# A hybrid attention and RG-LRU encoder layer: sixteen pairs of weight tiles in seven products, and one more high part made by ScalarE

## The reference

```python
proj = einsum('bsd,de->bse', x, w_in) + b_in          # x is 1024 x 1024
q, k, v, g_attn, x_rnn, g_rnn, m_attn, m_rnn = split(proj)
attn = window_attention(rope(q), rope(k), v, sink) * silu(g_attn)      # 8 heads, |i-j| <= 128
xc   = centred_depthwise_conv(x_rnn, conv_w, conv_b)                   # width 4, 10 blocks of 128 channels
r, i = sigmoid(xc @ wa + ba), sigmoid(xc @ wx + bx)                    # per block, two directions
a    = exp(-8 * r * softplus(-lam));  u = sqrt(1 - a*a) * i * xc
rnn  = (scan_forward(a, u) + scan_backward(a, u)) * silu(g_rnn)
merged = sigmoid(m_attn) * (attn @ w_branch_attn) + sigmoid(m_rnn) * (rnn @ w_branch_rnn)
x = layernorm(alpha * x + merged @ w_out + b_out)
```

## Time and profile before

| | us |
|---|---|
| median of 3 runs (lowest to highest) | 1029.85 (1028.64 to 1030.46) |
| the profiled execution | 1029.07 |
| its span | 1027.3 |
| TensorE, GpSimd, VectorE, ScalarE busy in the span | 1009.8, 618.0, 670.9, 471.8 |

### The profile page before, as it was taken

One profiled execution on the slowest core, in us unless ns is written; L12 is line 12 of the kernel. 1 busy time (PEld: TensorE's weight loads), 2 busy tenths in 40 slices (PEclk: granted clock), 3 DMA queues, 4 the chain that ended last, 5 costly groups with the idle time before them and its releaser, 6 DMA issues.

```text
span 1027.3 us, 12975 instructions
## 1 busy us (share of the span) xinstructions
PE 1009.8 (98%) x4641; PEld 836.1 (81%) x4641; DVE 670.9 (65%) x769; ACT 471.8 (46%) x687; POOL 618.0 (60%) x378
## 2 busy tenths in 40 slices
PE   8999999999999999999999999999999999999997
PEld 6888888888888888878887888787887878888885
DVE  4946665503556653666587886877878488839756
ACT  4054445221554465573758466574856741102021
POOL 5654435446543422535499999999999734485223
PEclk9999999999999999999999999999999999999999
DMA  8264333565524121435262534435243788937012
GB/s 330 98 240 134 126 120 113 178 239 187 168 78 163 53 71 52 143 106 192 65 218 76 154 102 136 130 115 164 84 142 84 242 296 322 341 99 295 1 47 118
DMA packets 65861, 154.69 MB, mean 151 GB/s; under 512 B 6928, under 2 KB 7312, under 8 KB 65680
## 3 DMA queue, kind: packets, MB, share of 16 engines
q1 hardware_dynamic: 56880, 131.36, 38.7%
q10 hardware_dynamic: 8928, 22.64, 5.7%
HBM read 108.88 MB, written 45.09 MB: 150 GB/s over the span
## 4 chain that ended last, share of the span: by engine, by line
PE 83%; POOL 7%; DVE 4%; issue 3%; DMA 2%; ACT 1%; SPq 0%; DVEq 0%; POOLq 0%; ACTq 0%
PE proj L863 13%; PE proj L865 13%; PE proj L864 13%; PE proj L1067 6%; PE proj L1071 5%; PE proj L1073 5%; POOL w_lo L751 5%; PE aux L863 3%; PE aux L865 3%; PE aux L864 3%; PE aux L927 3%; PE aux L909 2%; POOL w_hi L764 2%; PE proj L1184 1%; PE proj L1183 1%
## 5 line engine op out<-in xcount | busy, mean ns | idle before, releaser
L716 POOL TENSOR_SCALAR w_hi<-raw 128x1024 fp32r<-128x1024 f32 (+1 forms) x46 | 62.5, 1358 | 246.1 <-PE proj L863 190.4
L863 PE MATMUL proj<-xt_hi,w_hi 128*128 128x512 f32 x476 | 192.2, 404 | 0.2
L865 PE MATMUL proj<-xt_hi,w_lo 128*128 128x512 f32 x476 | 186.4, 392 | 0.0
L864 PE MATMUL proj<-xt_lo,w_hi 128*128 128x512 f32 x476 | 186.2, 391 | 0.0
L751 POOL TENSOR_TENSOR w_lo<-raw,w_hi 128x512 fp32r<-128x512 f32 x66 | 123.7, 1879 | 4.4
L719 POOL TENSOR_TENSOR w_lo<-raw,w_hi 128x1024 fp32r<-128x1024 f32 (+1 forms) x46 | 123.4, 2682 | 3.8
L865 PEld LDWEIGHTS proj<-xt_hi,w_lo 128*128 128x128 f32 x476 | 89.3, 188 | 19.7
L863 PEld LDWEIGHTS proj<-xt_hi,w_hi 128*128 128x128 f32 x476 | 89.6, 188 | 15.7 <-DVE xt_lo L1604 0.8
L864 PEld LDWEIGHTS proj<-xt_lo,w_hi 128*128 128x128 f32 x476 | 89.6, 188 | 14.1
L1067 PE MATMUL proj<-xt_hi,w_hi 128*128 128x512 f32 x224 | 87.8, 392 | 1.5 <-POOL w_lo L751 1.5
L1073 PE MATMUL proj<-xt_hi,w_lo 128*128 128x512 f32 x224 | 87.2, 389 | 0.0
(11 more groups left out here) (199 smaller groups left out, 2467.6 us busy)
## 6 DMA issues: line engine op xcount, KB each, us to landing
raw<-stream SPq DMA_DIRECT2D x52, 512.0 KB, 4.2
presum_a<-stream SPq DMA_DIRECT2D x42, 256.0 KB, 2.9
sums<-presum_a SPq DMA_DIRECT2D x42, 256.0 KB, 2.0
raw<-sums SPq DMA_DIRECT2D x38, 256.0 KB, 2.8
spill<-part ACTq DMA_DIRECT2D x16, 512.0 KB, 3.1
merges<-stage_out ACTq DMA_DIRECT2D x32, 256.0 KB, 3.6
raw<-stream SPq DMA_DIRECT2D x31, 256.0 KB, 2.7
raw_half<-stream SPq DMA_DIRECT2D x21, 256.0 KB, 2.8
```

What stands on the lines that cost most here:

```text
L716: nc.gpsimd.tensor_scalar(hi, raw[:, raw_slot, cols], 1.0, 0.0, ALU.mult, ALU.add)\
L863: begun = nc.tensor.matmul(bank, wh, mov_hi, start=first, stop=False)
L864: nc.tensor.matmul(bank, wh, mov_lo, start=False, stop=False)
L865: return begun, nc.tensor.matmul(bank, wl, mov_hi, start=False, stop=last)
```

## The change

`PLAIN` goes from 3 to 1. The units x3, g1, x4 and g2 become two more x/g pairs; the first pair of all is no longer a merge pair but (x3, g1), and 16 pairs are 8 x/g and 8 merge pairs. The order of the first blocks is written anew on each engine (four branch tiles before gates(1,0); in block 2 TensorE runs products 0 to 3 of its x/g pair between gates(2,0) and gates(2,1), in the later blocks product 0 alone as before). The sums of weights have 32 parts in place of 28. `BY_ACT` gets product 6 of each x/g pair, and products 2 to 6 of the very first; in the loop over blocks ScalarE makes this copy behind decay_exp and early_copy(q,2). GpSimd makes the gate weights behind product 6 for the first two x/g pairs and behind product 3 else, as before. The last loads (`load_branch(0)`, the states) wait for two more splits.

```diff
...
-PLAIN = 3
-TWINS = [(("merge", 0, 0), ("merge", 0, 1))]
+PLAIN = 1
+TWINS = []
 for _b in range(PLAIN, RNN_BLOCKS):
     if _b < RNN_BLOCKS - 1:
         TWINS.append((("x", _b + 2) if _b < RNN_BLOCKS - 2 else ("g", _b + 1), ("g", _b)))
-    TWINS.append((("merge", _b - 2, 0), ("merge", _b - 2, 1)))
+    if _b > PLAIN:
+        TWINS.append((("merge", _b - 2, 0), ("merge", _b - 2, 1)))
...
-BY_ACT = tuple(7 * q + i for q in MERGES[:-1] for i in (4, 5, 6))
+BY_ACT = tuple(7 * q + i for q in range(len(TWINS) - 1)
+               for i in ((2, 3, 4, 5, 6) if q == 0 else (4, 5, 6) if q in MERGES else (6,)))
...
+_hosts = [u for u in range(FIRST_PRESUM, UNIT_B) for _ in range(2 if u in (4, 6, 8, 10, 12, 19, 21, 23, 24, 25) else 1)]
+for _n, _part in zip(_hosts, [(q, part) for q in range(len(TWINS)) for part in range(2)]):
+    PRESUMS[_n].append(_part)
...
@@ -587,11 +585,11 @@
                 ks = slice(2 * c, 2 * c + 2)
                 sp.dma_start(home[3][:, ks, :], moving[:, k + 2 * c:k + 2 * c + 2, cols]).then_inc(t_landed[step], 16)
 
-            for name in NAMES_B[:10]:
+            for name in NAMES_B[:6]:
                 load_unit(name)
-            for step in range(6):
+            for step in range(2):
                 load_t(step)
-            for name in NAMES_B[10:]:
+            for name in NAMES_B[6:]:
                 load_unit(name)
...
@@ -631,11 +629,13 @@
                 for i in range(7):
                     load_half(7 * q + i)
                     if i == 3 and q == 0:
+                        for step in range(2, 6):
+                            load_t(step)
+                    if i == (2 if q else 5) and q not in MERGES:
+                        load_gates(TWINS[q][1][1] + 1)
+                    if i == 5 and q == 0:
                         load_t3(0)
                         load_t3(1)
-                        load_gates(PLAIN)
-                    if i == 2 and q not in MERGES:
-                        load_gates(TWINS[q][1][1] + 1)
...
-            sp.wait_ge(product_split, PRODUCTS - 4)
+            sp.wait_ge(product_split, PRODUCTS - 2)
...
             def twin_weights(q, gates_of):
 
                 for i in range(7):
                     split_half(7 * q + i)
-                    if i == 3 and gates_of:
+                    if q == 0 and i == 1:
+                        t1_low()
+                    if i == (6 if q < 2 else 3) and gates_of:
                         gate_weights_half(gates_of)
...
-            for b in range(RNN_BLOCKS):
-                if b != PLAIN:
-                    gates(b, 0)
-                if b < 2:
-                    branch(b, 0)
-                if b >= PLAIN:
-                    twin_product(merge_of(b) if twin_of(b) is None else twin_of(b), 0)
-                if b == PLAIN:
-                    twin_product(twin_of(b), 1)
+            gates(0, 0)
+            branch(0, 0)
+            gates(0, 1)
+            for t in range(1, 5):
+                branch(t // 4, t % 4)
+            gates(1, 0)
+            branch(1, 1)
+            gates(1, 1)
+            branch(1, 2)
+            branch(1, 3)
+            rnn_tile(("x", 2), 0)
+            for i in range(7):
+                twin_product(0, i)
+
+            for b in range(PLAIN + 1, RNN_BLOCKS):
+                first = merge_of(b) if twin_of(b) is None else twin_of(b)
+                early = 4 if b == PLAIN + 1 else 1
+                gates(b, 0)
+                for i in range(early):
+                    twin_product(first, i)
                 gates(b, 1)
-                if b < 2:
-                    for t in range(1, 4):
-                        branch(b, t)
-                if b in (1, 2):
-                    rnn_tile(("g", b), 1)
-                if b < PLAIN:
-                    rnn_tile(("x", b + 2), 0)
+                for i in range(early, 7):
+                    twin_product(first, i)
                 if twin_of(b) is not None:
-                    for i in range(2 if b == PLAIN else 1, 7):
-                        twin_product(twin_of(b), i)
-                if b >= 2:
-                    for i in range(1 if b == RNN_BLOCKS - 1 else 0, 7):
-                        if b == PLAIN - 1 and i == 6:
-                            gates(PLAIN, 0)
+                    for i in range(7):
                         twin_product(merge_of(b), i)
...
-                act.wait_ge(product_begun, n - 2)
+                act.wait_ge(product_begun, max(1, n - 2))
                 copy(w_slot(n)[0], half_slot(n % N_SLOTS)).then_inc(act_hi_done, 1)
...
 
             silu_gate(0)
             act.wait_ge(attn_split, 2 * N_HEADS + 2)
-            for b in range(RNN_BLOCKS):
+
+            pad_x(1, FILLS["x", 1])
+            sigmoids(0, 0)
+            conv_begin(1, FILLS["x", 1])
+            spill_tile(0)
+            sigmoids(0, 1)
+            decay_tanh(0)
+            conv_high(1)
+            decay_exp(0)
+            decay_square(0, 0)
+            spill_tile(1)
+            decay_square(0, 1)
+            roots(0)
+            for t in range(2, 5):
+                spill_tile(t)
+            t_high(0)
+            t_high(1)
+
+            act.wait_ge(rnn_done, 1)
+            sigmoids(1, 0)
+            store_state(0)
+            spill_tile(5)
+            sigmoids(1, 1)
+            decay_tanh(1)
+            decay_exp(1)
+            spill_tile(6)
+            decay_square(1, 0)
+            spill_tile(7)
+            decay_square(1, 1)
+            roots(1)
+            for step in range(2, 6):
+                t_high(step)
+            pad_x(2, FILLS["x", 2])
+            high_weights(0, 2)
+            conv_begin(2, FILLS["x", 2])
+            early_copy(0, 0)
+            high_weights(0, 3)
+            t3_high(0)
+            high_weights(0, 4)
+            t3_high(1)
+            early_copy(0, 1)
+            high_weights(0, 5)
+            high_weights(0, 6)
+            conv_high(2)
+            early_copy(0, 2)
+            early_copy(0, 3)
+            sigmoid_of(1)
+
+            for b in range(PLAIN + 1, RNN_BLOCKS):
                 last_one = b == RNN_BLOCKS - 1
                 q, m = twin_of(b), merge_of(b)
-                if b > PLAIN:
-                    early_copy(m - (2 if q is not None else 1), 3)
-                if b < PLAIN:
-                    pad_x(b + 1, FILLS["x", b + 1])
-                if b:
-                    act.wait_ge(rnn_done, b)
+                merge_before = merge_of(b - 1)
+                if merge_before is not None:
+                    early_copy(merge_before, 3)
+                if b == PLAIN + 1:
+                    early_copy(q, 0)
+                act.wait_ge(rnn_done, b)
                 sigmoids(b, 0)
-                if b >= PLAIN:
-                    merge_gate(m - (2 if q is not None else 1), 2)
-                    merge_gate(m - (2 if q is not None else 1), 3)
-                if q is not None:
+                if b == PLAIN + 1:
+                    store_state(PLAIN)
+                if merge_before is not None:
...
                     early_copy(m, 0)
                 if not last_one:
-                    conv_begin(b + 1, FILLS["x", b + 1] if b <= PLAIN else None)
-                spill_tile(b, 0)
+                    conv_begin(b + 1, None)
                 sigmoids(b, 1)
                 if q is not None:
                     early_copy(q, 1)
                 if last_one:
                     early_copy(m, 1)
                 decay_tanh(b)
-                if b == 2:
-                    t_high(3)
                 if not last_one:
                     conv_high(b + 1)
                 decay_exp(b)
-                if q is not None:
-                    early_copy(q, 2)
-                if last_one:
-                    early_copy(m, 2)
-                if b == 2:
-                    silu_gate(b)
+                early_copy(m if last_one else q, 2)
+                if not last_one:
+                    high_weights(q, 6)
                 decay_square(b, 0)
...
+                early_copy(m, 0)
+                high_weights(m, 4)
+                sigmoid_of(b)
+                early_copy(m, 1)
+                high_weights(m, 5)
+                high_weights(m, 6)
+                early_copy(m, 2)
+                merge_gate(m, 0)
+                store_state(b)
+                merge_gate(m, 1)
...
+            gated_input(1)
+            one_less_decay(1, 0)
+            one_less_decay(1, 1)
+            scan_input(1)
+            t_low(3)
+            t_low(4)
+            t_low(5)
+            for tap in range(1, CONV_W):
+                conv_tap(2, tap)
+            t3_low(0)
+            t3_low(1)
+            conv_low(2)
+            scans(1)
+            for number in range(4):
+                twin_sum(0, number)
+            state_sum(1)
+            silu_of(1)
+            gated_state(1)
+
```

(80 more changed lines are left out.)

100 lines of the change are left out of this document (32 added, 68 removed).

## The result

| | before | after |
|---|---|---|
| median, six runs each (lowest to highest), us | 1029.02 (1028.32 to 1030.46) | 1046.26 (1044.82 to 1046.94) |
| the profiled execution; its span | 1029.07; 1027.3 | 1045.77; 1044.0 |

The ratio is 1.0164, 95% interval 1.0154 to 1.0174: 17 us slower, with 24 matmuls fewer. The forecast was 10 us slower; the time lies in the range.

What follows compares the result with a forecast made beforehand. TensorE, busy 98%, was taken as the bound, with GpSimd and a ScalarE/VectorE chain nearly level. M6 of block 8 at 529.9 + 6 x 45.8 = 804.7, not 794.85, gave +9.8 us: 1039.6 us, range 1027 to 1047.

Steps and rivals of the forecast that it cites:

- Attention and weight sums: Four more parts of weight sums in attention, in GpSimd's and SP's queues: taken as costing nothing.
- First blocks: From gates(0,0) at 394.80 to block 2 at 479.1 with no waits, tile t1 ready near 459.
- Block 2: ScalarE's copy behind decay_exp makes P6 start 5.9 us late and M6 at 529.9, not 519.9: 10 us lost.
- Blocks 3 to 8: GpSimd waits for ScalarE's late copy of P6, so six turns take 45.8 us each.
- loop A: In blocks 3 to 8, the closed loop over GpSimd through the new wait: 45.1 to 46.5 us a turn.
- the rival in which TensorE falls behind: Only block 2 stalls; later the copy comes in time, turns 44.2 to 45.1; 1030 to 1035.5 us, chance 0.14.
- The chain alone, 44.3 + 0.5: Chain of ScalarE and VectorE plus the new copy in blocks 3 to 8: 44.8 us, lower end of the turn.
- The end: Block 9 and last loads: no x/g pair, loads still two products ahead of use; nothing gained or lost.
- The signs: Seven GpSimd waits for ScalarE's w_hi, 3 to 4 us in blocks 3 to 8, about 11 in block 2, among others.
- Faster: GpSimd relieved by 1.6 us a turn, TensorE sets turns of 43.53; 1022.0 us, chance 0.14.
- M0 locked out: GpSimd's M0 copy beside one_less_decay, 0.98 more, loop A 46.1 to 47.5; with t1 rival 1042 to 1050, chance 0.12.
- the main case: Slower as forecast, turns of 45.2 to 46.6 us, total 1035.5 to 1044.5 us, chance 0.57.

Runs made afterwards that it cites:

- e11: e7 with the ten attention units hosting two parts of weight sums changed to 16 to 25; 1033.72 us.
- e1: Changed kernel with the high part of product 6 made by GpSimd again in all x/g pairs but the first; 1029.73 us.
- e3: Changed kernel with product 6's copy given back to GpSimd in blocks 3 to 8, kept on ScalarE only in block 2; 1033.93 us.
- e2: Changed kernel with product 6's copy given back to GpSimd in block 2 alone; 1041.48 us.
- e4: Changed kernel with ScalarE's copy of product 6 moved right behind decay_tanh, ahead of conv_high; 1029.76 us.
- e9: Kernel before, fourteen pairs, with ScalarE making product 6's copy of its six x/g pairs late, behind early_copy(q,2); 1039.61 us.
- e8: e1 plus a same-size ScalarE copy that nobody reads, where the change has its copy; 1030.34 us.
- e10: Kernel before, fourteen pairs, with the six ScalarE copies of product 6 right behind decay_tanh, ahead of conv_high; 1027.55 us.
- e7: e4 with block 2's early copies and high part ahead of gates(2,1)'s sigmoids, last twin sum behind gated_input, merge_gate(3) and early_copy(q,0) behind conv_begin; 1027.05 us.

## Why the prediction was right, and where it was off

The direction, the mechanism and the place were right. By its own steps, on the profiled executions (predicted span 1038.9 - 1.8 = 1037.1, measured 1044.0, so 6.9 us are missing):

**Attention and weight sums: taken as nothing, measured 2.2.** gates(0,0) starts at 396.97 in place of 394.80. Some 1.5 of it are the first head group (200.1 for 198.6 us), shown by e11 to come from the hosts of the sums; there TensorE waits 2.0 us for VectorE's q_lo and neg_max, 1.1 before. The rest is at the start of the execution, where single profiles of the variants differ as much or more. This step failed: it looked only at GpSimd's idle time behind the sums, not at VectorE beside them.

**First blocks: right.** Block 2 starts 481.32 - 396.97 = 84.35 us after gates(0,0), 84.3 predicted; no wait, and t1 is in time.

**Block 2: +10 forecast, +12.7 measured, and the cause half right.** gates(0,0) to gates(3,0) is 140.56 us, 137.9 by the forecast (M6 at 529.9 and its 2.82), 2.6 more. Two waits for GpSimd of 0.72 and 0.50 us at P0 and P1 were not foreseen; the copy's end came 8.0 us after the second sigmoid's (8.3 to 9.1 forecast); from there to M6 25.7 against 24.5. P6 waited 5.27 us, 5.9 forecast. What failed is the sub-step that gave the whole stall to the copy: e1 has none and still loses 8.2 us, because early_copy(q,2) is as late and P6 needs it too. The copy adds 2.6 (e3 against e1) to 5.4 us (the changed kernel against e2) to block 2.

**Blocks 3 to 8: 45.8 forecast, 46.1 measured per turn, +1.7 in six.** Between loop A's 45.1 and 46.5, with the loop shown by e2, e3, e4 and e9. But 46.1 is a mean, and no turn has it: the rival in which TensorE falls behind and the copy then comes nearly in time is true of every second turn or so (44.4 us, GpSimd's wait 1.5 to 1.8), and the turn after it pays 47.4 to 48.0 (wait 3.88). I read it so: a long turn leaves TensorE late at the gates, ScalarE starts its sigmoids late against GpSimd, and so on by turns. No run isolates that, and why two long turns follow each other in blocks 6 and 7 stays open.

**The chain alone, 44.3 + 0.5: wrong.** e8 puts 0.5 us more on it and the turn stays. It was only the lower end.

**The end: +0.4.** From gates(9,0) on it is 1044.0 - 814.03 = 229.97 us, 229.6 forecast. These are 2.2 + 2.6 + 1.7 + 0.4 = 6.9, the whole difference.

**The signs.** GpSimd's waits for ScalarE ahead of P6 are seven, as forecast, but 8.6 us in block 2 in place of 11, and 1.5 to 3.9 us behind it in place of 3 to 4.

**The rivals.** Faster: its condition, a copy that ends before 595.1 in the turn of the earlier trace rows, did not hold, but e4 and e10 make it true, and e4 is 16.5 us better than the changed kernel, e10 12.1 better than e9. Neither reaches the 1022 that the rival gave: in e4 block 2 still takes 52.12 us, attention its 2.2, and the turns are 43.5 to 44.6 us. M0 locked out: its condition held. GpSimd's copy for M0 takes 1.59 or 1.60 us in all six turns (the row at 604.72), 0.62 in five of the six before (596.41 in the earlier trace rows). But M2's copy, 1.60 us in those five, takes 1.06 or 0.62 here, so that GpSimd's work from M0's copy to M6's low part is 20.8 us in the turns of 44.4 (578.97 - 558.15 in block 3) and 21.6 in the long ones (626.31 - 604.72 in block 4), with 20.7 before; e2 and e9 show the same two lengths turn for turn. In e4 M0's copy takes 1.59 us in five of six turns too, and the turns stay at 43.5 to 44.6. So in GpSimd's own time the lock-out is 0.9 us of a long turn, which is 3.0 to 3.6 longer than a short one. The time, 1046.3, lies outside the 1035.5 to 1044.5 of the main case and inside the 1042 to 1050 of this rival, but it is attention and block 2 that put 4.8 us of it there, not a turn of 46.1 to 47.5.

## What to carry to other kernels

Moving a small copy to an idle engine moves it into that engine's order. Ask not how busy the engine is but behind what the copy will stand and who waits for it in order: here a copy of 0.6 us in each of six turns, on an engine busy 46%, cost the old kernel 10.5 us at one place (e9) and gained 1.6 at another some five us earlier in its stream (e10). When a stall is put down to a new instruction, look whether the consumer has another input from the same place in the same stream. And work that fills an idle engine may be paid by a third one, whose instructions take longer beside it (e11: 100.9 us in place of 89.4).

## What the runs showed of the hardware beside this

TensorE came out of a wait of 5.27 us at half its clock. Its timeline and two windows of the changed kernel (the granted clock stands behind the busy times):

```profile
511.59 0.63 PE L1081 MATMUL proj<-xt_hi,w_lo 128*128 128x512 f32 x1
512.02 0.63 PE L1075 MATMUL proj<-xt_hi,w_hi 128*128 128x512 f32 x1
512.44 0.63 PE L1079 MATMUL proj<-xt_lo,w_hi 128*128 128x512 f32 x1
```

```profile
504.00:510.00 6.00, 1.33 (x6) 0.75 (x4) 1.22 (x1) 5.96 (x7) 0.81 (x1) 0.80 0.00 0
510.00:516.00 6.00, 4.76 (x12) 3.50 (x12) 3.91 (x3) 1.66 (x2) 5.83 (x5) 0.63 0.15 45
```

The starts are 0.43 us apart in place of 0.2267, the 1.2 GHz level, for nearly all of nine matmuls, which took about 1.8 us more. It cost little here, since M0 waited for GpSimd again (1.06 us at 516.43). In e7 the same level followed a wait of only 2.11 us, six matmuls behind it (the granted clock was 1.00 from 810 to 821 us and 0.51 from 823 to 826):

```profile
821.21 0.47 PE L871 MATMUL aux<-xt_hi,w_hi 128*128 128x512 f32 x1 [2.11 <-issue]
...
822.79 0.63 PE L871 MATMUL aux<-xt_hi,w_hi 128*128 128x512 f32 x1
823.22 0.63 PE L872 MATMUL aux<-xt_lo,w_hi 128*128 128x512 f32 x1
```
